# Hybrid encoder trunk in fp32: each layer opens with one 288-column operand of o and gate columns, chunk 0 is transposed raw, the second layer's first loads are asked for in the last expert, and read-outs and keys are shared between the two scan directions

## The reference

```python
h = _rmsnorm(x, mix_norm[l])
aq, ak, av, sz, sxbc, sdt, mq, mk, mv, mo, mi, mf = jnp.split(h @ w_in[l], offsets, axis=-1)
ya = _window_attention(...)      # 4 heads, 2 kv heads, window 128
yb = _ssd_mixer(sz, sxbc, sdt, ...)   # conv over 5 tokens, silu, then a scan in both directions
yc = _mlstm_mixer(mq, mk, mv, mo, mi, mf, ...)   # 4 heads, both directions, gated by sigmoid(mo)
x = x + jnp.concatenate([ya, yb, yc], axis=-1) @ w_out[l]
x = x + _expert_choice_ffn(_rmsnorm(x, ffn_norm[l]), router[l], w_gate[l], w_up[l], w_down[l])
```

```python
a_cs = jnp.cumsum(a, axis=-1)
cb = jnp.einsum('bclhn,bcshn->bhcls', Cc, Bc) * jnp.exp(_segsum(a))
y_diag = jnp.einsum('bhcls,bcshp->bclhp', cb, xdt)
y_off = jnp.einsum('bclhn,bchpn,bhcl->bclhp', Cc, prev, jnp.exp(a_cs))   # the read-out of the carried state
```

## Time and profile before

| | us |
|---|---|
| median of 3 runs | 2414.69 |
| lowest and highest | 2413.03, 2416.08 |
| the profiled execution | 2412.42 |
| its span in the trace | 2411.0 |
| PE busy in it | 2336.8 |
| DVE, ACT, POOL busy | 1046.9, 585.4, 538.1 |
| mean granted clock of TensorE, as a share of full speed | 0.991 |

### The profile page before, as it was taken

One profiled execution on the slowest core, in us unless ns is written; L12 is line 12 of the kernel. 1 busy time (PEld: TensorE's weight loads), 2 busy tenths in 40 slices (PEclk: granted clock), 3 DMA queues, 4 the chain that ended last, 5 costly groups with the idle time before them and its releaser, 6 DMA issues.

```text
span 2411.0 us, 34301 instructions
## 1 busy us (share of the span) xinstructions
PE 2336.8 (97%) x13630; PEld 1683.5 (70%) x13630; DVE 1046.9 (43%) x1961; ACT 585.4 (24%) x1265; POOL 538.1 (22%) x550
## 2 busy tenths in 40 slices
PE   7999999999999999999889999999999999999998
PEld 4577578874555788877645775788745468888786
DVE  4851566596645111111148515665965451111111
ACT  3220232344332111111132202323443321111111
POOL 1011453144211111111110114531442111111111
PEclk9999999999999999999999999999999999999999
DMA  3102222121227988778331012221212279887783
GB/s 131 38 18 70 71 90 81 62 97 53 79 76 268 327 289 280 265 262 287 92 121 38 18 65 76 80 78 62 97 54 79 79 270 329 286 281 258 269 287 79
DMA packets 149344, 352.24 MB, mean 146 GB/s; under 512 B 9885, under 2 KB 38049, under 8 KB 149186
## 3 DMA queue, kind: packets, MB, share of 16 engines
q1 hardware_dynamic: 134210, 308.11, 35.5%
q0 software_dynamic: 14976, 41.95, 7.0%
HBM read 307.75 MB, written 42.28 MB: 145 GB/s over the span
## 4 chain that ended last, share of the span: by engine, by line
PE 86%; DVE 7%; DMA 2%; ACT 2%; issue 1%; POOL 1%; SPq 1%; DVEq 0%; POOLq 0%; ACTq 0%; PEldq 0%
PE ps L1724 81%; DVE SCR L1168 2%; PE ps L2268 1%; PE ps L2015 1%; ACT SCR L1001 1%; DVE MID L1294 1%; DVE TMP L1168 1%; PE ps L2078 1%; DMA SCR<-cs_rows 1%; PE ps L1740 1%; DVE SCR L1177 1%; DMA SCR<-m_rows 0%; DVE HT L1168 0%; DMA HT<-h_sample,idxs 0%; PE ps L1933 0%
## 5 line engine op out<-in xcount | busy, mean ns | idle before, releaser
L1724 PE MATMUL ps<-MID,HT 128*128 128x512 f32 (+2 forms) x2240 | 608.4, 500 | 2.9 <-PE ps L1724 2.9
L1724 PE MATMUL ps<-HT,MID 128*128 128x160 f32 (+2 forms) x4192 | 575.4, 304 | 5.2 <-DVE HT L1168 5.2
L1724 PEld LDWEIGHTS ps<-HT,MID 128*128 128x128 f32 (+1 forms) x4192 | 560.4, 190 | 25.2 <-issue 23.9
L1724 PE MATMUL ps<-RING,HT 128*128 128x256 f32 (+2 forms) x2080 | 466.7, 391 | 2.5 <-DVE RING L1172 1.3
L1724 PEld LDWEIGHTS ps<-RING,HT 128*128 128x128 f32 (+1 forms) x2080 | 372.8, 190 | 85.9 <-issue 37.1
L1724 PEld LDWEIGHTS ps<-MID,HT 128*128 128x128 f32 (+1 forms) x2240 | 231.4, 151 | 227.3 <-issue 206.0
L1724 PE MATMUL ps<-HT,RING 128*128 128x512 f32 (+1 forms) x960 | 353.6, 526 | 0.0
L1177 DVE SCALAR_TENSOR_TENSOR HT<-HT,ps 128x160 f32<-128x160 f32 (+1 forms) x128 | 40.8, 319 | 683.2 <-ACT HT L1132 658.6
L1724 PEld LDWEIGHTS ps<-HT,RING 128*128 128x128 f32 x960 | 181.3, 192 | 160.7 <-issue 153.1
L824 POOL DMA_INDIRECT y_prompt<-SCR,idxp x32 | 50.5, 1578 | 618.4 <-ACT SCR L1142 617.8
L1132 ACT ACTIVATE HT<-ps 128x160 f32<-128x160 f32 (+1 forms) x128 | 38.6, 302 | 520.4 <-PE ps L1724 512.4
(11 more groups left out here) (239 smaller groups left out, 2130.3 us busy)
## 6 DMA issues: line engine op xcount, KB each, us to landing
MID<-w_gate SPq DMA_DIRECT2D x32, 2048.0 KB
MID<-w_up SPq DMA_DIRECT2D x32, 2048.0 KB
MID<-w_down SPq DMA_DIRECT2D x32, 2048.0 KB
RING<-w_in SPq DMA_DIRECT2D x22, 1024.0 KB, 5.3
SCR<-cs_rows SPq DMA_DIRECT2D x20, 1024.0 KB, 5.2
SCR<-m_rows SPq DMA_DIRECT2D x20, 512.0 KB, 3.8
MID<-w_out SPq DMA_DIRECT2D x8, 1024.0 KB, 6.7
y_sample<-RING SPq DMA_DIRECT2D x16, 512.0 KB, 2.6
```

What stands on the lines that cost most here:

```text
L1724: return pe.matmul(out, a, b, start=start, stop=stop)
```

## The change

- The 256 o columns, the 16 mLSTM gate columns beside them and the 16 dt columns become one operand `OG` of 288 columns, loaded by two DMAs into the space that the SSD inputs use later. The layer starts with one unit per chunk (8 matmuls of 288 columns) between the transposes. `gates`, its copies and the `FOLD` products go; the o units at the end of the SSD loop go.
- Chunk 0 is transposed as loaded. ACT scales its o and gate rows while copying them out; for the other units DVE multiplies `hT` of chunk 0 by the roots, spread over the partitions by one matmul (`rs_spread`, `scale_first`).
- At the end of layer 0 SP asks in the last expert for the parameters and `OG` of layer 1, and for the two prompt chunks of x when the last prompt rows are scattered, before the engines meet.
- The SSD loop has two units per chunk. The read-out of the SSD state is 2 matmuls of 512 columns in place of 4 of 256, that of the mLSTM 4 of 130 in place of 8 of 65.
- Keys of a pair of chunks are turned once (5 pairs in place of 8 steps), ACT keeps them in SBUF, DVE weighs them from there.
- xbc units run feature by feature, and on DVE `conv(1)`, `conv(2)` and on ACT some copies stand elsewhere.

The order of names is the same up to the exponentials, but the tanh here waits for `conv(2)`, which DVE before did ahead of the running maxima and now does behind them:

```diff
                     for d in range(2):
                         tt(WS[:, :, d, :], TMC[:, :, d, :], SPV[:, :, 8 * d:8 * d + 8], ALU.mult, ws_made if d == 1 else dve_chain)
-                    conv(2)
+                    conv(1)
                     dve.wait_ge(urow_made, 1)
...
                     silu(1)
+                    conv(2)
                     dve.wait_ge(mcol_made, 1)
```

The core of the rest of the diff:

```diff
-SLICES = [("xbc", 1024), ("xbc", 1280), ("xbc", 1536), ("z", 512), ("z", 768), ("qk", 1808), ("qk", 2064),
-          ("v", 2320), ("o", 2576), ("att", 0), ("att", 256)]
+SLICES = [("og", 2576), ("xbc", 1024), ("xbc", 1280), ("xbc", 1536), ("z", 512), ("z", 768), ("qk", 1808), ("qk", 2064),
+          ("v", 2320), ("att", 0), ("att", 256)]
...
+                    def load_og(layer):
+                            for at, c0, w in ((0, 2576, 272), (272, 1792, 16)):
+                                sp.dma_start(OG[:, :, at:at + w], wi[layer * D:(layer + 1) * D, c0:c0 + w]
+                                             .rearrange("(k p) n -> p k n", p=P)).then_inc(og_loaded, 16)
...
                     if layer + 1 < DEPTH:
+                        sp.wait_ge(gu_made, KF * (E - 1) + 1)
+                        load_parameters(layer + 1)
+                        load_og(layer + 1)
+                        sp.wait_ge(gu_made, KF * E)
+                        sp.wait_ge(scattered_p, seen["scatter"] + 16 * E)
+                        for c in range(NP):
+                            x_load(c, layer + 1)
                         sp.wait_ge(layer_done, 8 * layer + 4)
...
                     else:
-                        load_parameters()
-                        ring_load(0)
-                        sp.wait_ge(scattered_p, seen["scatter"])
-                        for c in range(NP):
-                            x_load(c)
                         sp.wait_ge(scattered_s, seen["scatter"])
-                        for c in range(NP, NC):
-                            x_load(c)
+                    for c in range(NP, NC):
+                        x_load(c)
...
+                    def scale_first():
+                        dve.wait_ge(rs_spread, 1)
+                        first = hT[:, :, 0:P]
+                        tt(first, first, ps[:, 2, 0:P].unsqueeze(1).to_broadcast([P, KD, P]), ALU.mult, first_scaled)
...
-                            evac(U_QK + 3 * c + 1)
+                            evac(U_QK + 2 * c + 1)
                             if c + 1 < NC:
                                 ssd_exp(c + 1, 0)
-                            evac(U_QK + 3 * c + 2)
-                            if c + 1 < NC:
                                 ssd_exp(c + 1, 1)
...
-                    for c in range(4):
+                    turn_x(0)
+                    unit(0)
+                    pe.wait_ge(rooted, 1)
+                    mm(ps[:, 2, 0:P], rs[:, 0:1].to_broadcast([P, P]), ident).then_inc(rs_spread, 1)
+                    turn_x(1)
+                    for c in range(2, NC):
                         turn_x(c)
-                    pe.wait_ge(wg_loaded, 32)
-                    gates(0)
-                    unit(0)
...
+                        unit(c - 1)
+                    unit(NC - 1)
...
-                        for d in range(2):
-                            for g in range(2):
-                                last = mm(ps[:, 6 + g, 256 * d:256 * d + 256], BC[64 * g:64 * g + 64, 1, t:t + P],
-                                          PREV[64 * g:64 * g + 64, d, c, :])
+                        for g in range(2):
+                            last = mm(ps[:, 6 + g, :].rearrange("p (d n) -> p d n", d=2), BC[64 * g:64 * g + 64, 1, t:t + P],
+                                      PREV[64 * g:64 * g + 64, :, c, :])
...
-                        for u in range(U_QK + 3 * c, U_QK + 3 * c + 3):
+                        for u in range(U_QK + 2 * c, U_QK + 2 * c + 2):
                             unit(u)
```

More of the change, by code:

```diff
@@ L46 @@
     _i = [k for k, _ in SLICES[:_s]].count(_k)
-    if _s == 0:
-        UNITS += [(_s, _k, h, g) for g in range(3) for h in range(2)]
-    elif _k in ("xbc", "qk"):
+    if _k in ("xbc", "qk"):
         UNITS += [(_s, _k, 2 * _i + h, g) for h in range(2) for g in range(3)]
@@ L84, with pair_of @@
 STEPS = [i for i in range(NC) if has_next(i)]
+KEY_PAIRS = []
+for _i in STEPS:
+    _pair = (scan_chunk(0, _i), scan_chunk(1, _i))
+    if not any(set(_pair) == set(x) for x in KEY_PAIRS):
+        KEY_PAIRS.append(_pair)
+def pair_of(n):
+    c = scan_chunk(0, STEPS[n])
+    return next(i for i, x in enumerate(KEY_PAIRS) if c in x)
 def tcol(c):
@@ L566, in _ @@
                                      MROW[:, d, :].rearrange("p (c t) -> p c t", c=NC)).then_inc(mrow_stored, 16)
-                    for i in range(3, 7):
+                    for i in range(4, 8):
                         ring_load(i)
@@ L849, in square, with scale_x @@
                         act.wait_ge(x_loaded[c if c < 4 else 2 + c // 2], (seen["x"] + 16) * (1 if c < 4 else 2))
-                        link(act.activation(XSF[:, 0:D], XN[c], ACT.Square, accum_out=ss[:, c:c + 1]), squared)
-                    square(0)
-                    for c in range(NC):
-                        if c + 1 < NC:
-                            square(c + 1)
-                        if c % 2 == 0:
-                            act.wait_ge(rooted, c + 1)
-                            link(act.mul(XN[c], XN[c], rs[:, c:c + 1]), scaled)
+                        link(act.activation(XSF[:, KD * OGW:KD * OGW + D], XN[c], ACT.Square, accum_out=ss[:, c:c + 1]), squared)
+                    def scale_x(c):
+                        act.wait_ge(rooted, c + 1)
+                        link(act.mul(XN[c], XN[c], rs[:, c:c + 1]), scaled)
                     def evac(u):
@@ L903, in keep_xs @@
                                          ps[:, 2 + j % 2, 0:n * P].rearrange("p (c n) -> p c n", c=n), 0.5), xs_kept)
-                    evac(0)
-                    evac(1)
-                    act.wait_ge(par_loaded, 16)
+                    square(0)
+                    square(1)
+                    for c in range(2, NC):
+                        square(c)
+                        if c % 2 == 0:
+                            scale_x(c)
+                        if c >= 3:
+                            evac(c - 3)
+                    for u in range(NC - 3, NC):
+                        evac(u)
+                    act.wait_ge(par_loaded, 16 * (layer + 1))
                     link(act.activation(NEGA, pr("alog"), ACT.Exp), softplus_exp)
@@ L1269, in _ @@
                            cs_read if d == 1 else dve_chain)
-                    conv(1)
                     silu(0)
@@ L1811, in _ @@
                     last.then_inc(cs_made, 1)
-                    for u in range(6, 9):
-                        unit(u)
+                    xbc(1)
                     pe.wait_ge(cs_read, 1)
@@ L1840, in _ @@
                     turn_xs(1, 0, 2)
-                    unit(13)
+                    xbc(3, 1, 2)
                     turn_xs(1, 2, 3)
-                    unit(14)
+                    xbc(3, 2, 3)
                     pe.wait_ge(mcol_kept, 1)
```

267 lines of the change are left out of this document (130 added, 137 removed).

## The result

| | before | after |
|---|---|---|
| median, us | 2413.86 (4 runs, 2410.38 to 2416.08) | 2431.41 (4 runs, 2429.16 to 2433.72) |
| profiled execution, us | 2412.42, span 2411.0 | 2432.54, span 2431.1 |
| PE busy; not busy, us | 2336.8; 74.2 | 2347.5; 83.6 |
| mean granted clock | 0.991 | 0.982 |

After takes 17.6 us more than the four runs of before in the table. Against all 27 runs of the kernel before (median 2411.38) it takes 1.0083 of its time (95%: 1.007 to 1.0095), 20.0 us more. The prediction was 2418.7 with a range of 2408 to 2428: the direction of the forecast's sum (+4.0) was right, the size was not, and the time lies outside the range.

What follows compares the result with a forecast made beforehand. PE, busy 97% of the span, was taken as the bound. Terms -4.8 - 13.2 + 2 x 1.7 + 2 x 11.7 - 2 x 2.4 = +4.0 on 2412.42 gave 2416.4, with 2.3 for the median 2418.7; range 2408 to 2428.

Steps and rivals of the forecast that it cites:

- Start of layer 0: Layer 0 up to the xbc units: 25.6 us without the ten o units, against 30.4 before; gain 4.8.
- xbc: xbc stage: conv(2) now behind the running maxima makes PE wait anew, 1.5 to 1.8 us per layer, taken as 1.7.
- Start of layer 1: Layer 1's start: loads no longer stand behind the engines' meeting, first unit at 1206.3; gain 13.2 us.
- Rivals C and D: Chance 0.12 together: C, early loads come late, 2426.3; D, loads in the last expert don't help, layer 1 gains 5.
- Keys, read-outs: Shared parts, per layer: keys -1.4 us, mLSTM read-out -0.7, SSD read-out -0.3, together -2.4.
- Rival A: mLSTM loop: PE still sets the pace, each chunk gives 0.5 us, 2410.1; chance 0.22.
- SSD loop: SSD loop with two units per chunk: PE waits for DVE's weights; loss 11.7 us per layer, bounds 8.5 and 14.
- wait at P(0): SSD loop, where PE takes up the second chunk's products and first sum: wait 4.8 us, before 1.33; 3.5 of the loss.
- For a longer wait I add 1.5: SSD loop: the lower clock behind the first wait costs 1.5 us more, part of the 11.7.
- Rival B: SSD loop: the clock falls after each new wait, costing another 1.5 and 3 us per layer, 2427.7; chance 0.16.
- PE busy -18, idle +22: Whole kernel: PE's busy time falls by some 18 us and its idle time grows by some 22.
- The first chain does not change: SSD loop's head: DMA rows, mask, exponents, exponentials and weights keep their time, so P(0) stays at 249.28.

Runs made afterwards that it cites:

- e3: Changed kernel with extra 256-column products that nobody reads, where PE waits in the SSD loop (nine, eight and six of them): 2422.26 us.
- e4: Changed kernel with one unit of the next chunk between products and sum in SSD chunks 7 to 9: 2422.01 us.
- e11: Kernel of e5 with one DVE operation per SSD chunk left out (the gate's (tanh + 1) * z, so the output is another): 2406.61 us.
- e7: Changed kernel with the early loads of layer 1 undone, asked for behind the meeting of the engines: 2437.59 us.
- e8: Kernel before with the shared parts alone: five turns of keys with ACT's copies, joint read-outs of both directions in both loops: 2408.47 us.
- e5: Changed kernel with the load of weight slice 7 moved in SP's queue behind the row requests of chunks 0 and 1: 2414.12 us.
- e12: Kernel before with the load of weight slice 6 moved behind the row requests of chunks 0 and 1: 2407.82 us.
- e1: Changed kernel with three units per chunk given back to the SSD loop, six from the z phase, and slice 7's load moved behind chunk 2's rows: 2401.79 us.

## Why the prediction was wrong

- *Start of layer 0*, gain 4.8, and *xbc*, a new wait of 1.7: together -3.1, measured -2.7. First unit at 10.13 for 10.3. By the prediction's own count (a layer's start ends with the first xbc unit of the new order) the start gained 5.3. In layer 1 ACT's wait stands as predicted (next fence); in layer 0 PE had come to the lower clock ahead of that place (0.72 over 128 to 139, a 512 unit of 9.09 at 129.98), and the wait is hidden in it. In e3, e4 and e11, where that stretch is not there, a wait of 1.84 or 1.85 stands in both layers.

```profile
1350.08 0.41 PE L1812 MATMUL ps<-cstt,MID 128*128 128x128 f32 x2 [1.84 <-ACT MID L917]
```

- *Start of layer 1*, gain 13.2: the mechanism was right, the match of -12.6 with -11.5 is in part luck. The first unit begins 8.1 behind PE's end of layer 0 (predicted 8.5), but the last ends 61.3 behind it (59.2), with chunk 2's wait of 2.37 and two slow units on the way. By the same count the start gained 10.8, not 13.2. The xbc and z stages behind it should have lost 1.7 and gained 1.8: the *kernel before* has the slow stretch in layer 1 (0.73 over 1320.7 to 1331.5, a 512 unit of 9.06 for 7.03), where the changed one has none. Such a stretch is worth some 3 us, and it stands in one layer, in both or in none from one profiled kernel to the next, so it says nothing of the change. e7 shows the early loads at work. Rivals C and D fall with the first unit's place.
- *Keys, read-outs*: 1.2 for 1.4 and 1.6 and 0.3 for 0.7; e8 has 3.3 us for 4.8. Rival A falls. Where PE doesn't wait, a chunk of the mLSTM loop takes 6.9, which is under the 7.0 that the prediction had named, but this doesn't last: from the fourth chunk on layer 0 has 7.5 to 7.7 with waits for DVE of up to 0.84, and both layers have chunks of up to 9.4 in which a unit at the lower clock (0.69 over 1700.9 to 1706.3) takes 5.3 for 3.7. From there to the loop's end the mean is 7.7 in layer 0 and 7.8 in layer 1, where the kernel before has 7.8 and 7.7. One of the waits, and the read-out behind it, 0.72 where about 0.6 was forecast and 1.11 stood before:

```profile
502.34 1.97 PE L1757 MATMUL ps<-MID,SCR 128*128 128x65 f32 x16 [0.83 <-DVE TMP L1198]
504.24 0.72 PE L1757 MATMUL ps<-MID 64*128 64x130 f32 x8
```

- *SSD loop*, loss 11.7 per layer: **this term failed**: the mechanism, PE waiting for DVE's weights where cover is missing, was right, but the sum left out one wait, the sum's for DVE's reads of the last output, and priced the lower clock too small. Measured 17.3 and 19.5, 18.2 and 21.0 with the units behind it. The wait at P(0) was 4.38 and 4.49 for 4.8, P(1) to P(6) went without waits, the products of chunk 7 waited 1.09 and 1.14 for 0.5, and DVE's tail ran 13.5 to 14.6 for 13.8 (its fused operation took 0.69 behind the weights of chunks 7 and 8 and 1.46 behind those of chunk 6, the two values of the prediction's bounds). What was missing, in layer 0: (1) "P(c) the time when PE takes up products(c+1) and sum(c)" takes both as one; the sum waits 3.0 longer, for DVE's reads of the last output: +3.0 at the end of the loop, shown by e4. (2) "For a longer wait I add 1.5": chunk 1 came 1.8 later than that put it (18.4 behind P(0) for 16.6), and behind the waits in the tail, where the prediction had nothing for the clock, sum 9 and the two units took 0.7 and 0.9 more. These four make 6.4 of the 6.5 between 11.7 and 18.2. The read-out's -0.3, a term of its own, did not come: products and sum of a chunk take 3.41 before (341.65 to 345.06) and after (398.99 to 402.40). In layer 1 the loop after was just as long; the loop before was 1.8 shorter than in layer 0 (168.96 against 170.80), which the prediction had taken as equal.
- *Rival B*, the clock after each wait, 2427.7, came nearest to the time. Its mechanism is real (0.50 twice in the windows), but it is only a part: of the 6.4 above, in layer 0, the clock has 3.4 and the reads of the output 3.0. e3 and e4 gave 9.2 and 9.4 us, but each also takes away a part of what the other does, so they can't be added.
- *PE busy -18, idle +22*: measured +10.7 and +9.4. Work at half clock counts as busy for twice as long, so a busy time can't be read as work (sum 7: 3.65 and 2.08 for 2.00 and 1.13). The mean clock fell from 0.991 to 0.982, which is up to 22 us of this span, an estimate from the two means, and most of the 29 us between forecast and measurement.
- "The first chain does not change" was true and hid the question that mattered: why it is so long. Its head stood in SP's queue behind a load that had nothing to do with it, to be seen before the change too. e5 and e12 show its price with and without cover.

Not settled: how the 29.6 us of e1 divide between cover and queue, and how far the clock's part would go with the waits left as they are.

## What to carry to other kernels

Work that only fills PE's time beside another engine's chain is not free to move: add up that chain against the cover that is left, chunk by chunk, and look for slack to trade in a neighbouring stage before taking the cover away. For each instruction that will now come early, list every semaphore that it waits for, and not only the one that ended its wait so far. And look what stands in each in-order queue, the DMA-issuing one too, ahead of the first link of the chain: the cheapest microseconds here were a load and two exponentials standing behind work that they did not need.
